# Two hybrid mixers in which turning, evicting and splitting weights change places

## The chip, the cores and the metric

One NeuronCore of a Trainium2 chip runs the whole kernel. The metric is the device time of one execution in microseconds (us). Engines are called by the names of the profile: PE (TensorE), DVE (VectorE), ACT (ScalarE), POOL (GpSimd) and SP (SyncE, which issues the large transfers).

## The reference, cut to what matters

The input is 256 tokens of width 1024 and passes four layers, two of a first kind and two of a second. The change touches only the mixer of the first kind, which runs twice (l = 0 and l = 1; here mixer 0 and mixer 1):

```python
def hybrid_mixer(h, ...):
    proj = h @ w_in                     # 256 x 2216
    z, xs, bm, cm, dt, q_lat, kv_lat, k_pe, gu, gv = split(proj)
    xs, bm, cm = split(silu(causal_depthwise_conv(concat(xs, bm, cm)) + conv_b))
    dt = softplus(dt + dt_bias)
    y_ssd = gated_group_rmsnorm(ssd_scan(xs, bm, cm, dt, a_log, d_skip), z, ssd_norm_w)
    q = rms_norm(q_lat, q_norm) @ w_qb          # then rope on its last 32 of 96
    kv = rms_norm(kv_lat, kv_norm) @ w_kvb      # 4 heads, 64 keys and 64 values each
    y_mla = mla_attention(q, kv, rope(k_pe))    # causal, 4 heads
    y_gm = gelu(gu) * (tril(w_s) @ layer_norm(gelu(gv)) + b_s)
    return concat(y_ssd, y_mla, y_gm) @ w_out
```

Behind mixer 0 comes a dense feed-forward (SwiGLU), behind mixer 1 eight experts of which each token uses two. Then come the two layers of the second kind.

## The kernel before

**Weights.** All weights stream in blocks of 1 MB through a ring of six slots (`plan`, `NS = 6`). SP issues the transfer of block n as soon as the last use of block n - 6 is over, strictly in the order of the plan. Products are made in three parts from numbers split in two: ACT copies a block to its high half (`high_halves`, L1261, ring of three), DVE subtracts that from the block and has the low half (`low_halves`, L1944), written over the block itself, and PE multiplies high by high, high by low and low by high (L497 to L499). Modulation vectors (`ada_w` blocks) are not split: DVE multiplies and adds them (`gemv`, L1884, two instructions for each block), and does so in `low_halves` ahead of the first split block that follows them in the plan. Four of them in mixer 0 are taken by PE (`gate_block`, L525).

**Order.** There is no planner: each engine has a program written out by hand and runs it in order. A wait on a semaphore stands in front of an instruction and holds all that is queued behind it on that engine. `ahead(i)` is the block two after i, so each block's step splits the weights two blocks ahead.

**A mixer.** The columns of `w_in` come as blocks named by their first column: 1280, 1536 (time steps, latents, k_pe), 512, 768, 1024 (the features xs, bm, cm, transposed), 1792, 2048 (gu, gv), 0, 256 (z). A token block makes tokens by columns, and ACT evicts it (`token_block`, L1405 and L1407). A feature block makes columns by tokens; ACT evicts it (L1415) and begins the convolution (L1423), DVE adds three taps for each of two chunks (L2188), ACT applies Silu (L1427). The latents are normalised on DVE, transposed by PE (`latents_turned`, L769), evicted by ACT (L1446), projected by PE (`latents_projected`, L779, L782) and evicted by ACT to q, k and v (L1455, L1459, L1460). DVE rotates them (`roped`, L2159), PE turns the heads (L795), and DVE and ACT copy two groups of them each (L2218, L1465). `differences` makes the decay matrices (PE L821, DVE L2296, ACT L1510).

**Attention.** It is a generator, and each `next(mla)` is one step in each engine's program: scores of head i (PE L724, L725), mask, maximum (DVE L2126 to L2132), exponentials (ACT L1390, L1391); probabilities of head i - 2 turned (PE L702) and evicted (ACT L1374); values of head i - 3 (PE L714 to L716). Between these steps stand the work of the scan (L2305, L2318, L2331, L848, L856), the gates (Gelu L1492 on ACT; statistics, root and normalisation one half of the tokens after the other, L2258 to L2268 on DVE, L1266 on ACT) and the last input blocks. At the end PE transposes the gated and attended part (L579), for which the last thing needed is L2311 on DVE, and multiplies it by two blocks of `w_out` in full (L886), while DVE and ACT finish the scan's part.

**PSUM.** Four banks (`R`) are taken in turn by block products, turned latents, projections, turned heads, scores and so on (`psum`); whoever takes a bank waits until its holder four takes earlier is evicted ("free"). Three more (`R2`) serve decays and turned inputs in the same way.

Of the kernel before, what the change touches and what calls it, by code (L numbers as in the profile page):

```python
# [8 lines left out]
ALU = mybir.AluOpType  # L9
# [78 lines left out]
def hybrid_kernel(nc, a, out):  # L88
    ctx = ExitStack()
    with ctx:  # L90
# [384 lines left out]
        def tensor_program(pe):  # L475
# [254 lines left out]
            def mixer1(l, m):  # L730
# [514 lines left out]
        def scalar_program(act):  # L1245
# [149 lines left out]
            def mixer1(l, m):  # L1395
# [3 lines left out]
                def token_block(c0, n):  # L1399
                    high_halves(main, ahead(turn_of["win", l, c0]))  # L1400
                    summed(turn_of["win", l, c0])
                    act.wait_ge(*at(*M, "token", c0))
# [6 lines left out]
                def feature_block(c0):  # L1409
                    high_halves(main, ahead(turn_of["win", l, c0]))  # L1410
                    summed(turn_of["win", l, c0])
# [10 lines left out]
                    for k in (ch, ch + 1):  # L1422
                        act.activation(xv[:, k, :], xc[:, k, 0:256], ACT.Identity, bias=pA[:, pc + 24 + k:pc + 25 + k], scale=pA[:, pc + k:pc + k + 1]).then_inc(  # L1423
                            *main.act((*M, "conv begun", k)))
                    for k in (ch, ch + 1):
                        act.wait_ge(*at(*M, "conv", k))
                        act.activation(xv[:, k, :], xv[:, k, :], ACT.Silu).then_inc(*main.act((*M, "xv", k)))  # L1427
# [62 lines left out]
                def gates():  # L1490
                    act.wait_ge(*main.act.last())
                    act.activation(G2[:, :, :], P1[:, :, 424:936], ACT.Gelu).then_inc(*main.act((*M, "gelu")))  # L1492
                    for t in range(2):
                        sd((*M, "gv", t), stat(2, *M, "gv mv", t)[:, 1:2])
# [34 lines left out]

                token_block(1280, 256)  # L1530
                time_steps()
                token_block(1536, 256)
# [329 lines left out]
        def vector_program(dve):  # L1862
# [302 lines left out]
            def mixer1(l, m):  # L2165
# [87 lines left out]
                def gates():  # L2253
                    dve.wait_ge(*at(*M, "gelu"))
                    for t in range(2):
                        bs, mv = stat(6, *M, "gv bs", t), stat(2, *M, "gv mv", t)
                        gv = G2[:, t, 256:512]
                        dve.bn_stats(bs, gv).then_inc(*vec())  # L2258
                        settled()
                        dve.bn_aggr(mv, bs).then_inc(*vec())  # L2260
                        rstd((*M, "gv", t), mv[:, 1:2], 1, 1e-5)
                        settled()
# [822 lines left out]
```

## Time and profile before

| | us |
|---|---|
| median of 3 runs | 2162.19 (2161.97 to 2172.66) |
| the profiled execution | 2158.98 |
| its span in the profile | 2157.1 |
| PE busy | 1985.6 (92%) |
| DVE busy | 1678.9 (78%) |
| ACT busy | 1169.0 (54%) |

Mixer 0 lies at about 42 to 190 us, mixer 1 at about 430 to 560 us of the span. The page's slices show PE busy 6 to 8 tenths in parts of these and 9 in most others. The granted clock of PE is 1.00 at full speed and 0.50 at its lower level.

### The profile page before, as it was taken

Reading aid. Unit: us, or ns where it says so; the run is one execution under the profiler, and the core shown is the slowest. Engines: PE = TensorE matmul, PEld = TensorE weight load, DVE = VectorE, ACT = ScalarE, POOL = GpSimd, SP = SyncE. Lnnn points to the kernel's source line nnn. Section 1 sums busy time; section 2 is a strip of 40 time slices with the busy share of each in tenths; the row PEclk is TensorE's granted clock in tenths of the full one; section 3 lists DMA queues with packets and bytes.
Section 4 is the critical chain, followed back from the end, with each engine's and each line's share of the span. In section 5 each row is a group of like instructions: output and inputs, shape, how many; then the busy total and the mean of one; then the engine's idle time right before and its main releaser. Section 6 shows DMA issues by size and latency. Waiting matters only on the chain.

```text
span 2157.1 us, 28343 instructions
## 1 busy us (share of the span) xinstructions
PE 1985.6 (92%) x11530; PEld 1717.5 (80%) x11530; DVE 1678.9 (78%) x1765; ACT 1169.0 (54%) x1314; POOL 73.3 (3%) x121
## 2 busy tenths in 40 slices
PE   6878999978889999999999999967889999889999
PEld 6676898777568787888788888757779998779998
DVE  6675888877588889898889989889678896865444
ACT  3543334364367777777677767645553345655432
POOL 6001000000100000000000000000010000000000
PEclk9988999998899999999999999978889999989999
DMA  9743799842389999999999999937229995314552
GB/s 353 244 166 137 278 335 370 285 130 99 138 285 323 350 366 366 332 349 375 343 342 355 370 331 358 343 101 248 86 97 338 353 368 182 121 59 137 187 184 98
DMA packets 251208, 554.37 MB, mean 257 GB/s; under 512 B 10076, under 2 KB 75856, under 8 KB 251072
## 3 DMA queue, kind: packets, MB, share of 16 engines
q1 hardware_dynamic: 247252, 544.13, 70.8%
q0 software_dynamic: 3552, 8.29, 1.1%
q8 instruction: 94, 1.54, 0.3%
q14 instruction: 42, 0.34, 0.1%
q10 hardware_dynamic: 268, 0.07, 0.0%
HBM read 551.40 MB, written 1.05 MB: 256 GB/s over the span
## 4 chain that ended last, share of the span: by engine, by line
PE 71%; DVE 14%; ACT 7%; issue 4%; DMA 4%; SPq 0%; ACTq 0%; DVEq 0%
PE bank L497 21%; PE bank L498 21%; PE bank L499 21%; DVE ring_lo L1944 4%; ACT ring_hi L1261 3%; DMA ring<-in_w_in_dram 1%; PE bank L886 1%; DVE acc L1884 1%; DMA ring<-in_ada_w_dram 1%; PE bank L579 1%; PE bank L1086 1%; DVE XN L2188 1%; DMA ring<-in_ffn_w_dram 1%; DVE work L2126 1%; PE bank L548 0%
## 5 line engine op out<-in xcount | busy, mean ns | idle before, releaser
L1944 DVE TENSOR_TENSOR ring_lo<-ring,ring_hi 128x2048 fp32r<-128x2048 f32 x417 | 950.1, 2286 | 271.4 <-ACT ring_hi L1261 268.4
L1261 ACT ACTIVATE ring_hi<-ring 128x2048 fp32r<-128x2048 f32 x417 | 795.5, 1913 | 492.0 <-PE bank L499 240.6
L497 PE MATMUL bank<-hh,ring_hi 128*128 128x256 f32 x1152 | 332.9, 289 | 19.5 <-ACT QK L1455 8.8
L498 PE MATMUL bank<-hl,ring_hi 128*128 128x256 f32 x1152 | 330.8, 287 | 0.0
L499 PE MATMUL bank<-hh,ring_lo 128*128 128x256 f32 x1152 | 330.5, 287 | 0.0
L497 PE MATMUL bank<-ring_hi,hh 128*128 128x256 f32 (+2 forms) x672 | 219.4, 327 | 30.6 <-ACT PT L1405 10.0
L497 PEld LDWEIGHTS bank<-hh,ring_hi 128*128 128x128 f32 x1152 | 226.2, 196 | 24.2 <-issue 13.5
L499 PE MATMUL bank<-ring_hi,hl 128*128 128x256 f32 (+2 forms) x768 | 241.9, 315 | 0.0
L497 PE MATMUL bank<-ring_hi,hgh 128*128 128x512 f32 (+1 forms) x576 | 220.3, 382 | 8.9 <-DVE ring_lo L1944 3.5
L498 PEld LDWEIGHTS bank<-hl,ring_hi 128*128 128x128 f32 x1152 | 226.2, 196 | 0.7 <-issue 0.2
L499 PEld LDWEIGHTS bank<-hh,ring_lo 128*128 128x128 f32 x1152 | 226.1, 196 | 0.0
L499 PE MATMUL bank<-ring_hi,hgl 128*128 128x512 f32 (+1 forms) x576 | 216.3, 375 | 0.0
L498 PE MATMUL bank<-ring_lo,hgh 128*128 128x512 f32 (+1 forms) x576 | 216.2, 375 | 0.0
L498 PE MATMUL bank<-ring_lo,hh 128*128 128x256 f32 (+2 forms) x672 | 212.9, 317 | 0.0
L497 PE MATMUL bank<-ring_hi,uh 128*128 128x512 f32 x496 | 199.0, 401 | 7.0 <-DVE ring_lo L1944 5.9
L498 PE MATMUL bank<-ring_lo,uh 128*128 128x512 f32 x496 | 196.5, 396 | 0.0
L499 PE MATMUL bank<-ring_hi,ul 128*128 128x512 f32 x496 | 196.5, 396 | 0.0
L1884 DVE SCALAR_TENSOR_TENSOR acc<-ring,csil,acc 128x1024 f32<-128x1024 f32 x140 | 179.8, 1284 | 13.7 <-DMA ring<-in_ada_w_dram 7.4
L497 PEld LDWEIGHTS bank<-ring_hi,hh 128*128 128x128 f32 x672 | 140.0, 208 | 47.0 <-issue 35.8
L499 PEld LDWEIGHTS bank<-ring_hi,hl 128*128 128x128 f32 x768 | 154.9, 202 | 6.6
L498 PEld LDWEIGHTS bank<-ring_lo,hh 128*128 128x128 f32 x672 | 140.3, 209 | 5.0 <-issue 0.7
L497 PEld LDWEIGHTS bank<-ring_hi,hgh 128*128 128x128 f32 x576 | 108.1, 188 | 33.8 <-issue 4.7
(424 smaller groups left out, 2774.4 us busy)
## 6 DMA issues: line engine op xcount, KB each, us to landing
ring<-in_moe_w_dram SPq DMA_DIRECT2D x264, 1024.0 KB, 5.2
ring<-in_ada_w_dram SPq DMA_DIRECT2D x48, 1024.0 KB, 7.2
ring<-in_w_mod_dram SPq DMA_DIRECT2D x48, 1024.0 KB, 7.3
ring<-in_w_in_dram SPq DMA_DIRECT2D x40, 1024.0 KB, 6.3
ring<-in_ffn_w_dram SPq DMA_DIRECT2D x33, 1024.0 KB, 5.5
ring<-in_w_gate_dram SPq DMA_DIRECT2D x22, 1024.0 KB, 5.1
ring<-in_w_up_dram SPq DMA_DIRECT2D x22, 1024.0 KB, 5.1
ring<-in_w_down_dram SPq DMA_DIRECT2D x22, 1024.0 KB, 5.0
```

The source lines that it names most:

```text
L497: pe.matmul(ps, xh, wh, start=first, stop=False)
L498: pe.matmul(ps, xh, wl, start=False, stop=False)
L499: return pe.matmul(ps, xl, wh, start=False, stop=last)
L579: x = pe.transpose(ban[kk][:, 256 * i + 128 * t:256 * i + 128 * t + 128], src[:, t, 128 * kc:128 * kc + 128], ident)
L886: x = pe.matmul(Y[t][h][:, :], YT[:, 2 * i + k, 128 * t:128 * t + 128], w[:, c:c + 512], start=first and k == 0, stop=False)
L1086: x = pe.transpose(ps[:, 128 * c:128 * c + 128], U[:, 128 * c:128 * c + 128], ident)
L1261: act.activation(ring_hi[i % NH][:, 0:z], ring[n % NS][:, 0:z], ACT.Copy).then_inc(*s.hi(("hi", home(s, i), i)))
L1884: x = dve.scalar_tensor_tensor(v, w[:, k, :], csil[:, col:col + 1], v, ALU.mult, ALU.add)
L1944: dve.tensor_tensor(ring_lo[n % NS][:, 0:z], ring[n % NS][:, 0:z], hi, ALU.subtract).then_inc(*s.lo(("lo", home(s, i), i)))
L2126: dve.tensor_tensor(S, R.of(*A, "scores", i, c)[:, 0:384], mask, ALU.add).then_inc(*vec(("free", *A, "scores", i, c)))
L2188: dve.scalar_tensor_tensor(xv[:, k, :], xc[:, k, j:j + 256], col(j), xv[:, k, :], ALU.mult, ALU.add).then_inc(*vec((*M, "conv", k)))
```

## The change

Only the orders inside `mixer1` change, on PE, ACT and DVE, and the gates' normalisation.

- PE: `latents_turned` stands behind block 768 and `latents_projected` behind block 1024 and its gate block; block 1792 stands ahead of `heads_turned`.
- ACT: the eviction is separate from the splitting (`block`) and from the Silus (`feature_gates`). Block 768 is split ahead and evicted before the latents, block 1024 before the projections; each pair of Silus comes after these. Block 1792 comes ahead of the heads. The high halves that stood with blocks 2048, 0 and 256 (those of blocks 256, and of `w_out` 0 and 1) come later.
- DVE: `roped` stands behind the decays; `block("win", 1792)` ahead of the copies of the heads; `block("win", 2048)` two attention steps later; the blocks 0 and 256 behind the gates, the spatial weights and the first chunk's output.
- Gates: both halves of the tokens together, in two parts, `gates_spread` up to the variance and `gates` from the root on; one root on ACT for two columns.

```diff
@@ PE, mixer1
                 feature_block(512)
                 gate_block(1)
-                latents_turned()
                 feature_block(768)
                 gate_block(2)
-                latents_projected()
+                latents_turned()
                 feature_block(1024)
                 gate_block(3)
+                latents_projected()
                 decays()
                 differences(0)
+                token_block(1792, 256)
                 heads_turned()
-                token_block(1792, 256)
@@ ACT, mixer1: block(c0) is now its own function, taken out of token_block
+                def block(c0):
+                    high_halves(main, ahead(turn_of["win", l, c0]))
+                    summed(turn_of["win", l, c0])
...
                 feature_block(512)
+                feature_gates(512)
+                feature_block(768)
                 latents_turned()
-                feature_block(768)
+                feature_gates(768)
+                feature_block(1024)
                 latents_projected()
-                feature_block(1024)
+                feature_gates(1024)
                 decays()
                 differences(0)
+                block(1792)
+                token_block(1792, 256)
                 heads_turned()
-                token_block(1792, 256)
...
                 next(mla)
                 contents()
                 next(mla)
+                block(2048)
                 gates()
                 states()
                 token_block(0, 256)
                 next(mla)
+                block(0)
+                sd((*M, "gv"), stat(4, *M, "gv mv")[:, 1:4:2])
                 token_block(256, 256)
+                block(256)
                 next(mla)
@@ DVE, mixer1
+                def gates_spread():
+                    mv = stat(4, *M, "gv mv")
                     dve.wait_ge(*at(*M, "gelu"))
                     for t in range(2):
...
+                        x = dve.bn_stats(stat(6, *M, "gv bs", t), G2[:, t, 256:512])
...
+                        x = dve.bn_aggr(mv[:, 2 * t:2 * t + 2], stat(6, *M, "gv bs", t))
...
+                    dve.tensor_scalar(mv[:, 1:4:2], mv[:, 1:4:2], 1e-5, None, ALU.add).then_inc(*vec((*M, "gv", "var")))
+                def gates():
+                    mv, gv = stat(4, *M, "gv mv"), G2[:, :, 256:512]
+                    dve.wait_ge(*at(*M, "gv", "sd"))
+                    dve.reciprocal(mv[:, 1:4:2], mv[:, 1:4:2]).then_inc(*vec())
...
+                    dve.tensor_tensor(gv, gv, bc(gmr[:, 0, :].unsqueeze(1), [128, 2, 256]), ALU.mult).then_inc(*vec())
...
+                    dve.tensor_tensor(gv, gv, bc(gmr[:, 1, :].unsqueeze(1), [128, 2, 256]), ALU.add).then_inc(*vec((*M, "gv", 0), (*M, "gv", 1)))
...
                 feature_block(768)
-                roped()
                 feature_block(1024)
                 decays()
+                roped()
                 differences(0)
+                block("win", 1792)
                 heads_turned()
-                block("win", 1792)
                 mla = attention((*M, "mla"), mla_heads(l), MLA_SCALE)
                 next(mla)
                 differences(1)
                 next(mla)
-                block("win", 2048)
                 stepped_inputs()
                 next(mla)
                 decayed(0)
                 next(mla)
+                block("win", 2048)
                 skipped_inputs()
+                decayed(1)
+                gates_spread()
+                next(mla)
                 gates()
+                spatial_weights()
+                chunk_outputs(0)
                 block("win", 0)
-                decayed(1)
-                next(mla)
-                spatial_weights()
                 block("win", 256)
-                chunk_outputs(0)
                 next(mla)
```

## Rows read from the trace of the kernel before

**Rows 1.** The page: busy us, share of the span; then two costly groups of instructions.

```profile
PE 1985.6 (92%) x11530; PEld 1717.5 (80%) x11530; DVE 1678.9 (78%) x1765; ACT 1169.0 (54%) x1314; POOL 73.3 (3%) x121
...
L1944 DVE TENSOR_TENSOR ring_lo<-ring,ring_hi 128x2048 fp32r<-128x2048 f32 x417 | 950.1, 2286 | 271.4 <-ACT ring_hi L1261 268.4
```

**Rows 2.** Order of time, PE, mixer 0: start, duration, instruction, [idle before <- releaser].

```profile
88.48 0.55 PE L497 MATMUL bank<-hh,ring_hi 128*128 128x256 f32 x1 [4.39 <-ACT QK L1455]
...
108.82 0.55 PE L497 MATMUL bank<-ring_hi,hh 128*128 128x256 f32 x1 [3.74 <-DVE QK L2218]
...
115.96 0.38 PE L724 MATMUL bank<-QK 96*128 96x128 f32 x2
...
134.59 0.69 PE L714 MATMUL bank<-QK,work 128*128 128x64 f32 x2 [6.46 <-ACT work L1374]
...
154.03 0.55 PE L497 MATMUL bank<-ring_hi,hh 128*128 128x256 f32 x1 [4.16 <-ACT PT L1405]
...
169.69 1.81 PE L579 MATMUL bank<-cst,YK 128*128 128x128 f32 x8 [1.26 <-DVE YK L2311]
```

**Rows 3.** Order of time, PE, mixer 1.

```profile
470.58 0.55 PE L497 MATMUL bank<-hh,ring_hi 128*128 128x256 f32 x1 [4.39 <-ACT QK L1455]
...
485.27 0.36 PE L497 MATMUL bank<-ring_hi,hh 128*128 128x256 f32 x1 [3.17 <-DVE QK L2218]
...
491.10 0.39 PE L724 MATMUL bank<-QK 96*128 96x128 f32 x2
...
520.70 0.55 PE L497 MATMUL bank<-ring_hi,hh 128*128 128x256 f32 x1 [5.88 <-ACT PT L1405]
...
535.73 1.51 PE L579 MATMUL bank<-cst,YK 128*128 128x128 f32 x6 [1.26 <-DVE YK L2311]
```

**Rows 4.** Order of time, ACT, mixer 0, first part.

```profile
87.54 0.42 ACT L1427 ACTIVATE XN<-XN 128x256 f32<-128x256 f32 x1 [1.02 <-DVE XN L2188]
87.86 0.47 ACT L1455 ACTIVATE QK<-bank 128x384 f32<-128x384 f32 x1
...
89.66 1.36 ACT L1261 ACTIVATE ring_hi<-ring 128x1344 fp32r<-128x1344 f32 x1
100.06 0.69 ACT L1276 ACTIVATE gate<-bank,cst 128x512 f32<-128x512 f32 x1 [9.04 <-PE bank L531]
```

**Rows 5.** Order of time, DVE, mixer 0, first part.

```profile
89.30 0.90 DVE L2159 TENSOR_TENSOR PT<-QK,cst 128x128 f32<-128x128 f32 x4 [1.79 <-ACT QK L1455]
...
91.77 2.60 DVE L1884 SCALAR_TENSOR_TENSOR acc<-ring,csil,acc 128x1024 f32<-128x1024 f32 x2
...
102.76 2.96 DVE L2188 SCALAR_TENSOR_TENSOR XN<-YT,pA,XN 128x256 f32<-128x256 f32 x6 [6.92 <-ACT XN L1423]
...
105.93 2.15 DVE L2296 SCALAR_TENSOR_TENSOR gate<-bank,st,cst 128x128 f32<-128x128 f32 x8
108.00 1.27 DVE L2218 COPY QK<-bank 96x512 f32<-96x512 f32 x2
109.19 5.30 DVE L1884 SCALAR_TENSOR_TENSOR acc<-ring,csil,acc 128x1024 f32<-128x1024 f32 x4
```

**Rows 6.** Order of time, ACT, mixer 0, second part.

```profile
131.91 1.91 ACT L1261 ACTIVATE ring_hi<-ring 128x2048 fp32r<-128x2048 f32 x1 [8.16 <-DMA ring<-in_w_in_dram]
...
144.70 1.28 ACT L1492 ACT_TABLE_LOAD   x1
145.99 1.06 ACT L1492 ACTIVATE PT<-PT 128x1024 f32<-128x1024 f32 x1
```

**Rows 7.** Stretches, DVE alone: us, busy (instructions), PE's granted clock, DMA share, GB/s.

```profile
138.00:169.60 31.60, 20.24 (x43) 0.82 0.41 150
504.90:535.70 30.80, 22.61 (x45) 0.88 0.32 111
```

**Rows 8.** Stretches, PE alone: us, busy (instructions), granted clock, DMA share, GB/s.

```profile
110.00:113.00 3.00, 3.00 (x21) 0.70 0.00 0
155.00:158.00 3.00, 3.00 (x16) 0.50 0.94 320
```

More of the change, by code:

```diff
@@ L1409, in feature_block @@
                 def feature_block(c0):
-                    high_halves(main, ahead(turn_of["win", l, c0]))
-                    summed(turn_of["win", l, c0])
+                    block(c0)
                     ch = (c0 - 512) // 128
@@ L1424, in feature_block, with feature_gates @@
                             *main.act((*M, "conv begun", k)))
+                def feature_gates(c0):
+                    ch = (c0 - 512) // 128
                     for k in (ch, ch + 1):
@@ L1492, in gates @@
                     act.activation(G2[:, :, :], P1[:, :, 424:936], ACT.Gelu).then_inc(*main.act((*M, "gelu")))
-                    for t in range(2):
-                        sd((*M, "gv", t), stat(2, *M, "gv mv", t)[:, 1:2])
                 def decays():
@@ L1528, in out_block @@
                     summed(turn_of["wout", l, i])
+                block(1280)
                 token_block(1280, 256)
                 time_steps()
+                block(1536)
                 token_block(1536, 256)
@@ L2251, in time_steps_after @@
                     dve.scalar_tensor_tensor(av_, dt_, -1.0, bc(sstat[:, 80:88].unsqueeze(1), [128, 2, 8]), ALU.mult, ALU.mult).then_inc(*vec((*M, "a")))
-                def gates():
+                def gates_spread():
+                    mv = stat(4, *M, "gv mv")
                     dve.wait_ge(*at(*M, "gelu"))
                     for t in range(2):
[L2256 to L2262, printed above, removed]
-                        dve.tensor_scalar(gv, gv, mv[:, 0:1], mv[:, 1:2], ALU.subtract, ALU.mult).then_inc(*vec())
-                        settled()
-                        dve.wait_ge(*at("ws", l))
-                        dve.tensor_tensor(gv, gv, gmr[:, 0, :], ALU.mult).then_inc(*vec())
-                        settled()
-                        dve.tensor_tensor(gv, gv, gmr[:, 1, :], ALU.add).then_inc(*vec((*M, "gv", t)))
+                        x = dve.bn_stats(stat(6, *M, "gv bs", t), G2[:, t, 256:512])
+                    x.then_inc(*vec())
+                    settled()
+                    for t in range(2):
+                        x = dve.bn_aggr(mv[:, 2 * t:2 * t + 2], stat(6, *M, "gv bs", t))
+                    x.then_inc(*vec())
+                    settled()
+                    dve.tensor_scalar(mv[:, 1:4:2], mv[:, 1:4:2], 1e-5, None, ALU.add).then_inc(*vec((*M, "gv", "var")))
@@ new lines, in gates @@
+                def gates():
+                    mv, gv = stat(4, *M, "gv mv"), G2[:, :, 256:512]
+                    dve.wait_ge(*at(*M, "gv", "sd"))
+                    dve.reciprocal(mv[:, 1:4:2], mv[:, 1:4:2]).then_inc(*vec())
+                    settled()
+                    for t in range(2):
+                        x = dve.tensor_scalar(gv[:, t, :], gv[:, t, :], mv[:, 2 * t:2 * t + 1], mv[:, 2 * t + 1:2 * t + 2], ALU.subtract, ALU.mult)
+                    x.then_inc(*vec())
+                    settled()
+                    dve.wait_ge(*at("ws", l))
+                    dve.tensor_tensor(gv, gv, bc(gmr[:, 0, :].unsqueeze(1), [128, 2, 256]), ALU.mult).then_inc(*vec())
+                    settled()
+                    dve.tensor_tensor(gv, gv, bc(gmr[:, 1, :].unsqueeze(1), [128, 2, 256]), ALU.add).then_inc(*vec((*M, "gv", 0), (*M, "gv", 1)))
```

2 lines of the change are left out of this document (1 added, 1 removed).

## The prediction

> **What bounds the kernel now.** I read the page first, then the waits and the order of time of PE, ACT and DVE in the two first mixers. PE is busy 92% of the span [rows 1], so what can be won lies where it waits. In the first mixer it waits 4.39 us before the block at 88.48 (for ACT's eviction of q), 3.74 before 108.82 (for DVE's copy of the turned heads), 6.46 before 134.59 (for ACT's eviction of turned probabilities), 4.16 before 154.03 (for ACT's eviction of the z block) [rows 2]. The second mixer has three of them: 4.39, 3.17 and 5.88 [rows 3]; the 6.46 is missing there, as its weights are in time. None is work that PE lacks. Each is an in-order queue: ACT's eviction stands behind an activation that waits for DVE (the Silu at 87.54, 1.02 after its convolution was asked for, and only then the q eviction at 87.86, whose bank the block at 88.48 takes [rows 4]), or behind weight splitting: ACT's high halves at 131.91 waited 8.16 us for the transfer of the last input block, and all behind them on ACT waited too [rows 6]. Behind such waits PE's clock falls as well: granted 0.70 in 110 to 113 us and 0.50 in 155 to 158, which is 1.2 GHz [rows 8].
>
> The two mixers are each a chain in two parts, cut at the first scores of the attention (115.96 and 491.10 [rows 2, 3]). I call that moment T and follow the new order from row to row. All work behind a mixer (boundary, feed-forward, experts) is unchanged; its transfers are gated by slots of the ring that PE frees, so I let a gain pass on in full.
>
> **First part, mixer 0.** The feature block 768 comes before the turning of the latents, so by bank order (four banks taken in turn) block 1024 needs the bank of block 512, evicted long before, and no longer that of q: the 4.39 goes. PE runs 768 at 68.4, gate block, turning, 1024 from 78.5 to 84.3, gate block and its sums to 89.6, projections to 94.2 and block 1792 from about 96.6 to 102.4, which before ended at 116.1. PE is no more the bound. What is late next is ACT and DVE:
> - ACT: the high halves of 1792 end at about 81.0 (0.9 us earlier than before, as block 768 ends 0.8 earlier), eviction and the two first conv steps to 82.7, latents to 83.8, then the Silus of 768, which end at 88.0 as before since DVE's convolution sets them. High halves of 2048, 1.36, to 89.4 [rows 4]; two gate evictions of 0.7 (before they waited 9.04 for PE [rows 4]) to 90.8; block 1024 evicted, conv begun, 92.5; six evictions of q and kv, 2.4, to 95.0.
> - DVE: the convolution of 1024, 2.96, ran at 102.76 after 6.92 of waiting [rows 5]; now 91.9 to 94.8. Decay copies 0.6. The rotation, 89.30 to 91.77 [rows 5] = 2.5, now behind it: 98.0. Differences 2.15 [rows 5]: 100.1. Now the change puts the low halves of block 0 in front of the copies of the turned heads, and in front of those stand four modulation products, 5.30 [rows 5], and the halves, 2.29 [rows 1]: 107.7. Copies 1.27: 108.9.
>
> So T comes at 108.9 instead of 115.96: **7.1 us gained**. The 3.74 stall is replaced by one of 5 us before T, in which PE has nothing. Bounds for this term: if the four products were hidden, T would be 105 (block 1792 to 102.4, transposes 1.5, copy 1.3), 11 gained; if DVE's convolution were not earlier, T would be 119.6, 3.7 lost.
>
> **First part, mixer 1.** The same order, no gate blocks, two modulation products fewer in it. Silu of 768 ends at 470.0 as before; high halves 1.36, eviction and conv begun: 473.1; convolution of 1024 473.0 to 475.9; copies to 476.4; rotation 478.9; differences 481.0. ACT's exponentials of the differences end at 481.6, its high halves of block 0 (1.9) at 483.5, so DVE waits 2.5 us, low halves to 485.8, copies 487.1. The last key transpose waits also, for ACT's eviction of block 1792 behind these halves (484.2). T is 487.1 instead of 491.10: **4.0 us**. The 4.39 and 3.17 stalls go, and PE idles some 5 us ahead of T instead.
>
> **Second part.** Counted from T. Before, the gated output that PE's next transposes wait for (DVE, L2311) was done at 53.6 in mixer 0 (169.6) and at 44.5 in mixer 1 (535.6) [rows 2, 3]. Now:
> - Scores, differences and inputs turned need the same time; block 2048 ends at 10.0 (before at 126.0, likewise). ACT evicts it and the turned probabilities at once, since the high halves of block 256 stand two steps later: the 6.46 goes. Third mask at 11.0 instead of 22.0 in mixer 0.
> - ACT: exponentials of head 3 end at 17.9; high halves of block 256 (landed at 16, as before) 19.8; Gelu with its table load (1.28 + 1.06 [rows 6]) 22.2; states and the z block evicted by 23.2: PE, ready at 23.0, hardly waits, so the 4.16 and 5.88 go.
> - DVE is now the bound. From the third mask to the gated output it had 20.24 us of work in mixer 0 and 22.61 in mixer 1 [rows 7]. To that come the products and low halves moved behind the masks: 5.3 + 2.3 in mixer 0, 2.6 + 2.3 in mixer 1. The gates in one go save some 0.6 (ten instructions for fourteen, the last two of them 512 wide) and one round trip to ACT. Sums: 27.2 and 26.9. Waits in it: 2.0 for the contents evicted behind exponentials; for the root 0.3 in mixer 0, and 2.1 in mixer 1, where DVE asks at 25.9 and ACT has first the high halves of the output block (which land at 24.6) to 26.5, then 1.28 of table and 0.2; seams of 0.05 between dependent instructions, 1.0. From 11.0: **41.2 and 43.0**. Gains: 53.6 - 41.2 = 12.4 and 44.5 - 43.0 = 1.5.
>
> The last low halves of the output blocks (4.6 us) stay in front of the second chunk's output as they were; PE will stand there 4 to 6 us for L2311. Nothing behind hides it. The second half of the SSD path has 10 us of cover by the 32 products of L886, in the old order as in the new.
>
> **Clock.** New idle stretches of PE: some 5 us before T in both mixers, 4 and 6 us before the transposes of L579 where 1.26 stood [rows 2]. After 4 us of idling 155 to 158 ran at half [rows 8]: 1.5 us lost there for that window alone. Bounds for one such place: 0, as behind the 3.17 wait, where the next block ran at full speed, and 3.5. I take 1.8 at each T (it delays block 2048, on which the rest hangs), 1.0 and 0.5 more than before at L579: 5.1 in all. What is saved of low clock in the middle is inside the difference to 53.6 already.
>
> The Trainium skill, "TensorE: Matmul & The Clock Gate", What's actually happening, says that the throttled clock is the default state and activity releases it. By this rule idling moved is idling paid again, which speaks against this change; the trace agrees with 0.50 [rows 8]. Were each of the four stretches paid in full the gain would be 6 smaller.
>
> A load of tables before Gelu took 1.28 and the Gelu began 0.01 later (144.70, 145.99) [rows 6]. The Trainium skill, "ScalarE: Activation LUTs", What ACT_TABLE_LOAD costs, puts a switch of sets at about 2.66 us with its drain. By it the root would come 1.4 later in each mixer and the gain be 2.8 smaller; I go by the row. The count of loads stays the same.
>
> **Sum.** 7.1 + 4.0 + 12.4 + 1.5 = 25.0; less clock 5.1; less 2 for handoffs between engines that I stepped over, some twenty at 0.1: 18 us. The profiled execution took 2158.98 (span 2157.1), the median of the runs is 2162.19. The difference is between executions; I take the gain off the median: **2144**.
>
> **Rivals.**
> - A, part of it given back: DVE's new order (low halves ahead of copies) plus low clock eat the first part whole, and the second keeps 12.4 - 4. Then 7 to 9 us: 2154. For it: every moved wait has DVE behind it, at 78% busy over the kernel. Against: DVE idled 6.92 ahead of the convolution [rows 5], and it waited on ACT's 8.16 [rows 6] too: the work moved has these holes to go to.
> - B, more: the first part goes to its upper bound in mixer 0, since the slots free earlier, and clock costs little: 25 + 4 = 29: 2133.
> - C, slower: the queue of DVE before T. If the convolution of 1024 does not come earlier (a transfer of block 2048 or the gate evictions later than I have them; it decides at DVE's 102.76 against 91.9), rotation, differences, four products, low halves and copies in a row put T at 119.6, 3.7 later, and by the same sum 2.3 later in mixer 1 (convolution at 479.2 as before, T 493.4). With two deeper clock falls of 3.5 that is 13 lost; if then the halves of block 256 land as late as before and DVE has 7.6 more behind them, the second part gains nothing: 2175. Against: nothing in the new order feeds the convolution but block 1024, whose bank is free.
> - D, it doesn't do what it says: the wait for block 256's transfer (8.16) just moves to where its product stands, so that mixer 0's second part gains 6, not 12: 2150. Against: the new order asks for these halves at 17.9 after T and the transfer lands at 16.
>
> **Chances.** Forecast with its surroundings (2137 to 2150) 0.58; A 0.17; B 0.10; D 0.11; C 0.04. The range: 2136 to 2156. What counts as no change is within 0.5%, 10.8 us, so 2151.4 to 2173: that is A, part of the forecast's upper edge and of D: 0.18; slower 0.03; faster 0.79.
>
> **What would show it.** In the trace after: no wait of PE for L1455 and none of 6 us at L714; block 1792 before the heads; T near 109 and, in mixer 1, near 472 (487.1 less the 15 to 16 gained in mixer 0, 19.5 less its share of clock and handoffs); the L1405 waits under 1 us; new waits of PE for L2218 or the scores and, at L579, for L2311 of 4 to 6 us; granted clock 0.5 to 0.7 just behind T. Wrong it would be if ACT's high halves of block 2048 start later than 90, if DVE waits for an arrival before its four products, or if the masks of head 3 come later than 19 after T.

## The result, and the profile after

The changed kernel takes 2138.22 us (median of 4 runs, 2136.80 to 2143.60) against 2163.98 (4 runs) for the kernel before: ratio 0.9891, 95% interval 0.9873 to 0.9909, so some 24 us faster. I had forecast 2144 and a range of 2136 to 2156. The profiled execution is the slowest of the four: 2143.60 us, span 2141.8; against the profiled 2158.98 of before that is 15.4 less. The profiled execution of the kernel before is in turn faster than all four of its timed ones (2161.97 to 2172.66). The two medians lie 25.8 apart: 5.0 us of the gap come from the profiled execution before, 5.4 from the one after. Where those 5.4 went is asked below.

The line numbers of DVE and ACT have moved in the changed kernel: L2230 is L2218 of before (copies of the turned heads), L2334 is L2311 (gated output), L2354 is L2331 (addition of a chunk's output, `chunk_outputs`), L1956 is L1944 (low halves), L1896 is L1884 (modulation products).

PE's order of time in mixer 0 answers to [rows 2] (start, duration, instruction, [idle before <- releaser]). The waits of 4.39, 3.74, 6.46 and 4.16 us are gone; the first scores, T, come at 108.77 instead of 115.96 behind a new wait of 5.22, and the transposes L579 at 153.25 instead of 169.69.

```profile
102.91 0.31 PE L795 MATMUL bank<-cst,QK 128*96 128x128 f32 x1 [0.35 <-ACT PT L1409]
...
108.77 0.77 PE L724 MATMUL bank<-QK 96*128 96x128 f32 x2 [5.22 <-DVE QK L2230]
...
110.61 3.10 PE L821 MATMUL bank<-cst,sstat 128*128 128x128 f32 x14
...
134.87 0.39 PE L497 MATMUL bank<-ring_hi,hh 128*128 128x256 f32 x1 [1.03 <-DVE ring_lo L1956]
...
143.18 2.77 PE L848 MATMUL bank<-YT,gate 128*128 128x64 f32 x16 [1.36 <-DVE YK L2354]
...
148.37 3.62 PE L872 MATMUL bank<-PT 128*128 128x64 f32 x16
153.25 1.94 PE L579 MATMUL bank<-cst,YK 128*128 128x128 f32 x8 [1.26 <-DVE YK L2334]
```

PE in mixer 1, to [rows 3]. Where the waits of 4.39, 3.17 and 5.88 were, there is one of 3.08 before a projection, which the prediction did not have, one of 1.06 before T and one of 2.35 before L848. A fourth wait of before, 4.11 us at 452.64 for the normalised latents (DVE L2198), which the prediction did not count, has become one of 1.38 at 447.82 and one of 1.90 at 455.74. T to L579 is 43.3 us, before 44.6.

```profile
462.50 2.08 PE L782 MATMUL bank<-mlaw,PT 128*128 128x512 f32 x2 [3.08 <-ACT YT L1416]
...
477.51 0.46 PE L724 MATMUL bank<-QK 96*128 96x128 f32 x2 [1.06 <-DVE QK L2230]
...
509.83 3.68 PE L848 MATMUL bank<-YT,gate 128*128 128x64 f32 x16 [2.35 <-DVE YK L2354]
...
520.81 1.94 PE L579 MATMUL bank<-cst,YK 128*128 128x128 f32 x8 [1.26 <-DVE YK L2334]
```

DVE ahead of T in mixer 0, to [rows 5]: convolution of block 1024, rotation (from 95.28), differences, four modulation products, low halves, copies, without a hole.

```profile
92.10 2.96 DVE L2200 SCALAR_TENSOR_TENSOR XN<-YT,pA,XN 128x256 f32<-128x256 f32 x6
...
95.28 0.89 DVE L2171 TENSOR_TENSOR PT<-QK,cst 128x128 f32<-128x128 f32 x4
...
97.75 2.15 DVE L2319 SCALAR_TENSOR_TENSOR gate<-bank,st,cst 128x128 f32<-128x128 f32 x8
99.82 5.30 DVE L1896 SCALAR_TENSOR_TENSOR acc<-ring,csil,acc 128x1024 f32<-128x1024 f32 x4
105.04 2.28 DVE L1956 TENSOR_TENSOR ring_lo<-ring,ring_hi 128x2048 fp32r<-128x2048 f32 x1
107.24 1.28 DVE L2230 COPY QK<-bank 96x512 f32<-96x512 f32 x2
```

DVE at the end of mixer 0's row, ahead of L579: here it waits for PE.

```profile
152.03 1.12 DVE L2334 SCALAR_TENSOR_TENSOR YK<-bank,pA,PT 128x128 f32<-128x128 f32 x4 [1.67 <-PE bank L872]
```

DVE's busy time from the third mask to the gated output in each mixer, to [rows 7] (us, busy, PE's granted clock, DMA share, GB/s). It was 20.24 and 22.61; forecast 27.2 and 26.9.

```profile
121.70:153.20 31.50, 26.48 (x43) 0.86 0.70 251
488.60:520.80 32.20, 26.49 (x43) 0.82 0.36 131
```

PE's granted clock in the changed kernel in four stretches of mixer 0, to [rows 8]: it is 0.50 (1.2 GHz) behind the wait before T, again low behind the 1.36 before L848, and still low at L872 and up to L579.

```profile
109.00:112.00 3.00, 3.00 (x13) 0.50 0.00 0
112.00:115.00 3.00, 3.00 (x21) 0.75 0.00 0
...
144.00:147.00 3.00, 3.00 (x15) 0.53 0.92 331
150.00:153.00 3.00, 1.99 (x10) 0.50 0.00 0
```

### The profile page after: what moved, and what is told of

Same layout as the page of the kernel before. It is cut to its first block, busy times and chain, and to the rows that moved or that the text cites. A ratio compares the mean times of both kernels' runs of the same rounds, so it can differ in the third digit from the quotient of the medians.

```text
span 2141.8 us, 28331 instructions
## 1 busy us (share of the span) xinstructions
PE 1985.2 (93%) x11530; PEld 1716.7 (80%) x11530; DVE 1676.3 (78%) x1757; ACT 1169.2 (55%) x1312; POOL 72.7 (3%) x121
## 4 chain that ended last, share of the span: by engine, by line
PE 70%; DVE 14%; ACT 7%; DMA 5%; issue 4%; SPq 0%; ACTq 0%; DVEq 0%
PE bank L497 21%; PE bank L498 20%; PE bank L499 20%; DVE ring_lo L1956 4%; ACT ring_hi L1261 4%; DMA ring<-in_ffn_w_dram 2%; DVE acc L1896 1%; PE bank L886 1%; DMA ring<-in_w_in_dram 1%; DMA ring<-in_ada_w_dram 1%; PE bank L579 1%; PE bank L1086 1%; DVE XN L2200 1%; PE bank L548 1%; DVE work L2138 1%
## 5 line engine op out<-in xcount | busy, mean ns | idle before, releaser
L1956 DVE TENSOR_TENSOR ring_lo<-ring,ring_hi 128x2048 fp32r<-128x2048 f32 x417 | 950.0, 2286 | 270.5 <-ACT ring_hi L1261 267.8
L1896 DVE SCALAR_TENSOR_TENSOR acc<-ring,csil,acc 128x1024 f32<-128x1024 f32 x140 | 179.7, 1283 | 14.2 <-DMA ring<-in_ada_w_dram 7.7
```

The source lines that it names most:

```text
L1896: x = dve.scalar_tensor_tensor(v, w[:, k, :], csil[:, col:col + 1], v, ALU.mult, ALU.add)
L1956: dve.tensor_tensor(ring_lo[n % NS][:, 0:z], ring[n % NS][:, 0:z], hi, ALU.subtract).then_inc(*s.lo(("lo", home(s, i), i)))
```

## The experiments

All times are medians, each ratio is against the kernel before on the same chip in the same session (its median there was 2162.15 to 2163.98; the table has that of the first). The columns from the fourth on come from one profiled execution each. "T" and "L579" are read from PE's order of time as above. The table gives all runs; "FF" is the stretch from the feed-forward's first product to mixer 1's first.

| run | median us | ratio (95%) | T, mixer 0 | T to L579, mixer 0 | FF | T to L579, mixer 1 |
|---|---|---|---|---|---|---|
| before | 2163.98 | | 115.96 | 53.73 | 218.9 | 44.63 |
| changed | 2138.22 | 0.9891 (0.9873-0.9909) | 108.77 | 44.48 | 225.0 | 43.30 |
| first part only | 2150.99 | 0.9942 (0.9921-0.9964) | 108.07 | 56.85 | 217.9 | 45.52 |
| second part only | 2152.93 | 0.9949 (0.9930-0.9968) | 116.76 | 42.05 | 221.7 | 43.05 |
| changed again | 2140.39 | 0.9887 (0.9871-0.9904) | 108.33 | 44.15 | 220.6 | 45.93 |
| chunk first | 2137.04 | 0.9877 (0.9860-0.9895) | 107.74 | 42.08 | 219.1 | 43.02 |
| both late | 2127.13 | 0.9831 (0.9813-0.9848) | 109.00 | 39.79 | 220.0 | 38.64 |
| late lows | 2134.77 | 0.9863 (0.9841-0.9884) | 109.48 | 40.27 | 221.5 | 44.38 |
| ten products | 2137.52 | 0.9883 (0.9863-0.9903) | 112.34 | 41.92 | 217.4 | 42.99 |
| heads first | 2145.83 | 0.9923 (0.9897-0.9948) | 104.62 | 53.07 | 222.9 | 44.74 |
| spread | 2124.78 | 0.9824 (0.9811-0.9838) | 107.21 | 41.56 | 220.6 | 36.26 |
| five products | 2137.62 | 0.9888 (0.9872-0.9903) | 108.13 | 42.07 | 218.7 | 44.09 |
| old gates | 2144.74 | 0.9916 (0.9903-0.9930) | 108.38 | 47.07 | 222.5 | 47.54 |

**First part only.** Up to `heads_turned` the changed order, from T on that of the kernel before.

Against the changed kernel, with the functions `gates` of the kernel before and, on ACT, each `block` back inside its token block, ahead of the eviction:

```diff
 ACT             contents()
                 next(mla)
-                block(2048)
                 gates()
                 states()
                 token_block(0, 256)
                 next(mla)
-                block(0)
-                sd((*M, "gv"), stat(4, *M, "gv mv")[:, 1:4:2])
                 token_block(256, 256)
-                block(256)
...
 DVE             next(mla)
+                block("win", 2048)
                 stepped_inputs()
                 next(mla)
                 decayed(0)
                 next(mla)
-                block("win", 2048)
                 skipped_inputs()
+                gates()
+                block("win", 0)
                 decayed(1)
-                gates_spread()
                 next(mla)
-                gates()
                 spatial_weights()
-                chunk_outputs(0)
-                block("win", 0)
                 block("win", 256)
+                chunk_outputs(0)
```

> Only the first part of the change: latents turned and projected a block later, evictions ahead of the Silus, rotation behind the decays, block 1792 ahead of the heads; from the first scores on all is as before, high and low halves of block 256 too. Theory (the two parts are separate gains cut at the first scores T): T comes 7.2 us earlier in mixer 0 (108.8) and 4.3 more in mixer 1, as in the changed kernel; T to PE's transposes stays 53.7 and 44.6 us, with the waits of 6.5 (L714) and 4 to 6 (L1405) back. Gain 10 to 12 us, ratio about 0.995. Rival (the parts hang together, the second is what lets the first through, or the transfer of block 256 eats it): gain under 5.

**Second part only.** The reverse: the order of before up to the heads, the changed one behind. Against the changed kernel:

```diff
 PE              gate_block(1)
+                latents_turned()
                 feature_block(768)
                 gate_block(2)
-                latents_turned()
+                latents_projected()
                 feature_block(1024)
                 gate_block(3)
-                latents_projected()
                 decays()
                 differences(0)
-                token_block(1792, 256)
                 heads_turned()
+                token_block(1792, 256)
...
 ACT             feature_gates(512)
-                feature_block(768)
                 latents_turned()
+                feature_block(768)
                 feature_gates(768)
-                feature_block(1024)
                 latents_projected()
+                feature_block(1024)
                 feature_gates(1024)
                 decays()
                 differences(0)
+                heads_turned()
                 block(1792)
                 token_block(1792, 256)
-                heads_turned()
...
 DVE             feature_block(768)
+                roped()
                 feature_block(1024)
                 decays()
-                roped()
                 differences(0)
-                block("win", 1792)
                 heads_turned()
+                block("win", 1792)
```

> Only the second part: halves two steps later on ACT and DVE, gates together; up to the heads all is as before. Theory: T stays at 116 in mixer 0; T to the transposes of L579 falls from 53.7 to about 43 in mixer 0 (the changed kernel had 44.5 with PE cold for some 1.8 us behind T, which here has the block 1792 ahead of it) and from 44.6 to about 43 in mixer 1. Gain 11 to 13 us, ratio about 0.9945. Rival (the gain of the second part came from the first part's earlier release of ring slots): T to L579 stays above 49 in mixer 0, gain under 6.

Measured: 0.9942 and 0.9949; the two shortfalls, 0.0058 and 0.0051, add to 0.0109, and the whole change has 0.0109 and, again, 0.0113. By the times they are separate gains of about equal size, as the theory had it. The waits of the second part are back in the first run, 6.39 us at L714 and 4.50 and 5.87 at L1405. Beyond the forecast: with the first part alone T to L579 in mixer 0 grew from 53.73 to 56.85, and with the second alone it fell to 42.05, lower than the 44.48 of both. So the first part's earlier T goes with 2.1 to 3.1 us more behind T. The granted clock points at the cause: with the second part alone it is 1.00 behind T, where the changed kernel has 0.50. The runs with added products test that.

```profile
117.00:120.00 3.00, 3.00 (x26) 1.00 0.62 180
```

In mixer 1 this run has a cost that the table does not show: from its first product to T it took 63.3 us, 2.8 more than the kernel before with the same order there. The waits are all but the same (4.09, 4.39 and 3.17), but the clock behind them differs: 0.54 in 477.8 to 480.8 behind the 3.17, against 1.00 in 485.3 to 488.3 in the kernel before.

**The changed kernel again.**

> The changed kernel once more, for its spread. In the two profiles at hand the products of mixer 0 end 16.4 us earlier, yet mixer 1 begins only 9.3 earlier: 7 us went in the dense feed-forward between them. Theory (the loss is the transfers' own variation from execution to execution): the stretch from the first product of the feed-forward to the first of mixer 1, 218.9 us in the trace before and 225.0 in the one after, is near 219 in this one. Rival (a price of the change: the feed-forward is bound by transfers and cannot be entered earlier): it is near 225 again. Time 2137 to 2140 either way, ratio 0.989.

Mixer 1 differs between the two executions of the changed kernel. In the first PE waits 1.06 us before T and runs at 1.00 behind it, the second scores come 2.52 us behind T, and T to L579 is 43.30. In this one it waits 2.60, runs at 0.50, the second scores come 4.83 behind T, and T to L579 is 45.93.

```profile
472.31 0.77 PE L724 MATMUL bank<-QK 96*128 96x128 f32 x2 [2.60 <-DVE QK L2230]
```

PE's stretches behind T in mixer 1, this execution and, below, the first one of the same kernel:

```profile
472.30:475.30 3.00, 2.98 (x12) 0.50 0.00 0
...
477.50:480.50 3.00, 2.99 (x24) 1.00 0.53 216
```

FF is 220.6, neither 219 nor 225. Over all thirteen profiles it lies between 217.4 and 225.0, and 225.0, that of the changed kernel's first profile, is the largest. Kernels with mixer 0 even shorter (both late) have 220.0. A price of the change of 6 us in every execution is ruled out by that; a price of 1 to 2 us can't be excluded, as the one profile of the kernel before has 218.9. That the variation is the transfers' own is argued, not shown.

**Chunk first.**

```diff
                 next(mla)
-                gates()
                 spatial_weights()
                 chunk_outputs(0)
+                gates()
                 block("win", 0)
```

> The changed kernel with spatial_weights and chunk_outputs(0) ahead of gates on DVE, where DVE waits for the root (1.04 us in mixer 0, 3.01 in mixer 1). Theory (PE's waits of 1.36 and 2.35 us for L2354 and the low clock behind them come from the bank that chunk_outputs(0) frees late): these waits go, L848 behind them takes 1.95 instead of 2.77 and 3.68, and the transposes of L579 come 1 to 3 us earlier in mixer 0 (where DVE had waited 1.67 for L872) and about 1.3 in mixer 1, where DVE's row of work stays the bound. Gain over the changed kernel 2 to 4 us. Rival (DVE's total is all that counts): 0 to 1.

The wait before L848 went and L848 ran in 1.95; instead PE stood 3.51 us at L579, so DVE's row of work is the next bound. From the start of L848 to the end of L872 PE took 5.2 us, in the changed kernel 8.8. T to L579 is 2.1 to 2.4 shorter than in the changed kernel in mixer 0. In mixer 1, where the second scores came 4.16 behind T (low clock), the 43.02 is to be held against the 45.93 rather than the 43.30: some 2.9 shorter, with PE standing 6.86 at L579. 0.9877 against 0.9887 in the same session: not told apart by timing.

```profile
141.12 1.95 PE L848 MATMUL bank<-YT,gate 128*128 128x64 f32 x16
...
149.82 1.94 PE L579 MATMUL bank<-cst,YK 128*128 128x128 f32 x8 [3.51 <-DVE YK L2334]
```

**Both late, and late lows alone.** Both late is chunk first and this (there `gates()` stands between `chunk_outputs(0)` and the two blocks):

```diff
                 chunk_outputs(0)
-                block("win", 0)
-                block("win", 256)
                 next(mla)
                 chunk_outputs(1)
...
                 late_features()
+                block("win", 0)
+                block("win", 256)
                 outputs()
```

> As the run with spatial_weights and chunk_outputs(0) ahead of the gates, and in addition the low halves of the two w_out blocks (and in mixer 1 the two modulation products ahead of them) stand on DVE behind late_features, not ahead of the second chunk's output. Theory (DVE's row of work up to L2311's place is what the transposes of L579 wait for, 3.5 us in mixer 0 and 6.9 in mixer 1 in that run): L579 comes 3 to 4.5 us earlier in mixer 0 and 5.5 to 7 in mixer 1, and the 32 products of L886 cover the 4.5 and 7.1 us moved behind. Gain over that run 8 to 11 us, ratio to the kernel before about 0.983. Rival (the cover is too short, the second transposes then wait for the scan's part): under 3 us.

> The changed kernel with only the low halves of the w_out blocks behind late_features; chunk_outputs(0) stays behind the gates. Theory: DVE is freed of 4.5 and 7.1 us, but PE's second within_chunk still waits for chunk_outputs(0) with the low clock behind it, so L579 moves 1 us or less earlier in mixer 0 (there DVE had already waited 1.67 for PE) and 1 to 3 in mixer 1. Gain 1 to 4 us over the changed kernel. Rival (DVE's total work is the bound alone): 4 and 7 us.

Both late has the time that was forecast, 0.9831, 10 us under chunk first, but not quite the terms. T to L579 is 2.3 shorter than in chunk first in mixer 0 (forecast 3 to 4.5) and 4.4 in mixer 1 (5.5 to 7); the rest came behind L579, where mixer 1 took 39.9 us up to its next stage instead of 43.0. The cover of L886 sufficed. Late lows alone gained 5 to 6 us by the ratio, above the forecast of 1 to 4. T to L579 is 40.27 in mixer 0, 4 us shorter, as its rival said: PE waited 1.07 us before L848, yet its clock stayed at 1.00, and L848 and L872 took 2.00 and 1.95 (in the changed kernel 2.77 and 3.62). Why the clock stayed up there is not shown. In mixer 1 it is 44.38: the late `chunk_outputs(0)` held PE for 2.73 us and L848 took 3.20. So in mixer 0 late lows do nearly all that both edits do (40.27 against 39.79); in mixer 1 it takes both (38.64).

**Ten products, five products.** Idle PE is kept busy before T:

```diff
                 heads_turned()
+                for _ in range(10 if l == 0 else 2):      # five products: 5 and 0
+                    pe.matmul(Y[0][0][:, :], ident, cst[:, 0:512], start=True, stop=True)
                 mla = attention((*M, "mla"), mla_heads(l))
```

> The changed kernel with products of 128x512 put on PE between the turned heads and the scores, ten in mixer 0 and two in mixer 1, written to a bank that nobody reads then; they add work, the outputs stay. Theory (idling before T costs low clock behind it, 2.4 us by the difference of 42.05 to 44.48 us from T to L579 between the run of the second part alone and the changed kernel): in mixer 0 the scores and differences behind T run at full clock, T to L579 is near 42, gain 2 us in the kernel. Rival (the 2.4 us came from elsewhere, such as DVE's row): T to L579 stays near 44.3.

> The changed kernel with five products of 128x512 on PE between the turned heads and the scores in mixer 0 only (they add work, the outputs stay), 0.87 us each by the run with ten, so that they end at 107.5 to 108, before T. Theory (low clock behind T costs 2.4 us): T stays at 108.3 to 108.8, the differences behind it take 1.95 us instead of 3.10, T to L579 is near 42. Gain 2 us over the changed kernel, which its timing alone hardly shows. Rival: T to L579 near 44.3.

Ten took 8.7 us (0.87 each) and ended behind the old T, so T came late, 112.34, but T to L579 fell to 41.92. Five ended in time: T 108.13, T to L579 42.07, the value of the second part alone, the differences L821 took 1.95 us, and the second scores came 2.52 us behind T instead of 4.78. In mixer 1, with the two products of the first of these runs in front of T, the second scores came 2.44 behind T.

```profile
108.13 0.46 PE L724 MATMUL bank<-QK 96*128 96x128 f32 x2 [0.49 <-DVE QK L2232]
...
108.86 1.95 PE L821 MATMUL bank<-cst,sstat 128*128 128x128 f32 x16
```

```profile
109.00:112.00 3.00, 3.00 (x28) 1.00 0.00 0
```

So work that nobody needs buys back 2.1 to 2.4 us (44.48 and 44.15 to 42.07): that is the price of low clock behind T in mixer 0. In the median it does not show (0.9888).

**Heads first.** On DVE:

```diff
                 differences(0)
-                block("win", 1792)
                 heads_turned()
+                block("win", 1792)
```

> The changed kernel with the two orders of block 1792 and the copies of the turned heads swapped on DVE. Theory (DVE's row, not T, is the bound in mixer 0): T comes 4 to 4.6 us earlier, at 104.2, but the first mask, which stands behind the four modulation products and the low halves, still comes at 110.5 to 111; L579 moves by less than 1 us either way in both mixers. Rival (T sets the end, as the sum of the prediction had it with its bound of 11 instead of 7 us): 4 us gained in mixer 0.

T came 4.15 earlier, as both expected, and the first mask at 111.47, half a microsecond behind what my theory had. But the kernel got slower than the changed one, by 5 to 8 us (0.9923 against 0.9887 and 0.9891; the intervals just overlap, and L579 of mixer 0 came 4.4 to 5.2 later in the profile), which neither had: PE, scores done, came to the transposes of the inputs and waited 5.56 us for a bank that DVE frees in `differences(1)`, behind the same products. Block 2048 then ran at half clock (granted 0.50 in each stretch from 115 to 127, with PE busy throughout), and all behind it was late. In the changed kernel DVE does the same products before T, and PE's wait is the one of 5.22 there.

```profile
104.62 0.46 PE L724 MATMUL bank<-QK 96*128 96x128 f32 x2 [0.77 <-ACT QK L1469]
...
113.96 1.11 PE L830 MATMUL bank<-cst,XN 128*128 128x128 f32 x4 [5.56 <-DVE gate L2319]
```

**Spread.** Both late, and in mixer 0 DVE's two products in front of the heads' copies go behind the second mask:

```diff
                 differences(0)
+                if l == 0:
+                    low_halves(main, ahead(turn_of["win", l, 1792]), False)   # without gemv
                 block("win", 1792)
                 heads_turned()
...
                 next(mla)
+                if l == 0:
+                    gemv(mods_left.pop(0))
                 stepped_inputs()
+                if l == 0:
+                    gemv(mods_left.pop(0))
                 next(mla)
```

> The best run so far (low halves of w_out late, chunk_outputs(0) ahead of the gates) and, in mixer 0 only, the two modulation products of DVE (four instructions, 5.3 us) taken out from in front of the copies of the turned heads: low halves of block 0 first, one product before stepped_inputs, one behind it, where DVE waited 1.5 and 2.0 us. Theory (these products set T in mixer 0 and PE's idling there costs clock behind it): T at 103.5 to 104 instead of 109.0, PE waits for L2230 under 1 us instead of 5.2, third mask 3 to 5 us earlier, L579 near 144 instead of 148.8. Gain 4 to 5 us over that run, about 2123. Rival (DVE's total is the bound and swallows it, as when the copies alone went ahead): under 1.5.

T came at 107.21, not at 103.5 to 104: DVE now waited 2.50 us for ACT's high halves of block 0, which stand behind ACT's exponentials, so the 5.3 us taken out brought T only 1.8 forward. L579 stayed (148.77 against 148.79). The 0.9824 against 0.9831 is inside the intervals, though it is the fastest median, 2124.78. The rival has the number right, but not the reason: at the end DVE waited 3.22 us for PE (L848), so its total was not the bound. PE began block 256 1.5 us earlier than in both late, but behind a wait of 2.39 instead of 1.03, at a granted clock of 0.63 instead of 1.00, and ended it at the same time (the next transposes start at 141.38, in both late at 141.40).

```profile
103.47 2.29 DVE L1956 TENSOR_TENSOR ring_lo<-ring,ring_hi 128x2048 fp32r<-128x2048 f32 x1 [2.50 <-ACT ring_hi L1261]
```

PE at the start of block 256, and its stretch behind that, in spread; the last line is the same place in both late:

```profile
134.04 0.39 PE L497 MATMUL bank<-ring_hi,hh 128*128 128x256 f32 x1 [2.39 <-DVE ring_lo L1956]
```

```profile
134.00:137.00 3.00, 2.96 (x16) 0.63 1.02 403
...
135.50:138.50 3.00, 2.95 (x24) 1.00 1.02 412
```

In mixer 1 the two kernels are the same, and T to L579 was 36.26 here and 38.64 in both late: the second scores came 2.51 behind T here and 4.83 there. That is the low clock behind T once more, 2.4 us.

**Old gates.** The functions `gates` of the kernel before at the new place, with a root for each half:

```diff
 ACT             block(0)
-                sd((*M, "gv"), stat(4, *M, "gv mv")[:, 1:4:2])
+                for t in range(2):
+                    sd((*M, "gv", t), stat(2, *M, "gv mv", t)[:, 1:2])
...
 DVE             decayed(1)
-                gates_spread()
                 next(mla)
                 gates()
```

> The changed kernel with the gates' normalisation as before, one half of the tokens after the other, in the place of the new one. Theory of the prediction (grouping saves 0.6 us of DVE's work and one round trip to ACT): DVE's stretch from the statistics to the last addition, 4.7 us in mixer 0 and 6.6 in mixer 1 in the changed kernel, grows by 2 to 3 us in each, and the transposes of L579 come 2 to 3 us later in each mixer; 4 to 6 us slower than the changed kernel. Rival (the root only waits behind ACT's high halves, with or without grouping): under 2.

T to L579 was 47.07 and 47.54, 2.6 to 2.9 and 1.6 to 4.2 longer than in the two profiles of the changed kernel; 0.9916 against 0.9887 and 0.9891, 5 to 6 us (the intervals just overlap). By these numbers grouping is about a quarter of the whole gain. The second trip to ACT explains little of it: DVE waited 0.27 us for it in each mixer. From the statistics to the last addition DVE took 6.0 us in mixer 0 instead of 4.7, so 1.3 more where 2 to 3 were forecast, 1.0 of it work and the seams of more instructions. The rest came through PE: it waited 2.69 us before L848 instead of 1.36, L848 took 3.21, the clock was 0.58 in 145 to 148 and 0.50 in 148 to 151, and DVE waited 2.12 for L872. In mixer 1 ACT's high halves ahead of the root waited 3.31 us for their transfer, 1.93 and 2.19 in the changed kernel, so part of the difference there is not the edit's.

## Why the prediction was right, and where not

- **T, mixer 0.** Forecast 108.9, measured 108.77, and by the chain as written: eviction and gate evictions earlier, then DVE's row without a hole. The bound of 105 for hidden products was wrong in kind: without them ACT's high halves are next (spread), and with the copies alone in front PE waits a step later (heads first).
- **T, mixer 1.** From its first product to T 60.5 before, 56.2 now: 4.3 gained, forecast 4.0. The step for PE failed, though: the last projection waited 3.08 us for the bank of block 1024, whose eviction the new order puts behind the Silus of 768. I had followed the bank only for block 1024 itself. It cost nothing in T, since DVE's row was later still: in all nine profiles with this order ahead of T, T came 56.2 to 56.3 us behind mixer 1's first product, with that wait at 3.07 or 3.08 in six of them and at 1.38 in three. In absolute time T was forecast near 472; it came at 477.51 in the first profile, with 6 us of that lost in FF, and at 472.31 in the second.
- **Second part.** The waits at L714 and L1405 went. L579 at 44.5 after T in mixer 0 (forecast 41.2 with 1.8 and 1.0 of clock, 44.0) and 43.3 in mixer 1 (43.0 with 2.3, 45.3). DVE's work was 26.5 in both for 27.2 and 26.9. The terms listed for mixer 0 add up to 41.5, not 41.2, so 12.1 gained and not 12.4. DVE waited 1.04 and 3.01 for the root, where I had 0.3 and 2.1: ACT's high halves ahead of it waited for the transfer of the output block in both mixers (2.21 and 1.93). A root ahead of these halves was not tried. The 43.3 is of the execution with full clock behind T; with low clock it was 45.93, so that mixer 1 agrees with 45.3 only when the clock falls, as I had charged it.
- **L579.** I had PE standing there 4 to 6 us for L2311. It stood 1.26, which in mixer 0 is little more than L2334 itself (1.12), begun when PE's own L872 was done. The step that failed is that PE arrives early: it waited before L848 for the bank that `chunk_outputs(0)` frees, and ran the rest at half clock (L848 2.77 and 3.68 for 1.95, L872 3.62 for 1.95), so that in mixer 0 DVE even waited 1.67 for PE. Chunk first brought PE's wait back, 3.51 and 6.86. The forecast of the whole hardly felt this miss, as DVE's row ended about where I had it.
- **Clock.** 1.8 at each T: 2.1 to 2.4 in mixer 0, shown by filling the idle time. In mixer 1 it varies between executions: of the nine profiles with the same order ahead of T, three ran the scores behind it at full clock (second scores 2.5 us behind T) and six wholly or partly at half (4.05 to 4.83); two pairs of equal code (spread and both late, the changed kernel twice) differ by 2.4 and 2.6 us from T to L579; five products, only partly at half clock there, has 0.8 more than the first of the changed kernel's two. The bound of 0, taken from the 3.17 wait, was one such case: behind the same wait the second part alone had 0.54. The other 1.5, charged at L579, fell due between L848 and L872 instead (3.6 us of PE in mixer 0 against chunk first). The "6 smaller" for all stretches paid in full has no sum behind it; at my bound of 3.5 a place, four places are 14, 8.9 more than charged. The granted clock in mixer 0 is 0.50 behind the wait and 1.00 with five products in it. The Trainium skill, "TensorE: Matmul & The Clock Gate", What's actually happening, takes the throttled clock as the default that activity releases; both rows agree with it.
- **Gates.** 0.6 us and a round trip, forecast inside the 12.4 and 1.5: worth 5 to 6 us of the kernel, of which the second round trip is 0.27 in each mixer and work and seams 1.0 in mixer 0; most of the rest is PE waiting longer and running at low clock behind that.
- **Sum.** The mixers gained 7.2 + 9.25 and 4.3 + 1.3 = 22.0 us in the two first profiles; the terms less clock were 25.0 - 5.1 = 19.9. The 2 us for handoffs were not needed. Of these 22 some 6 were lost in FF in that one execution, which is why its span fell only by 15.3; the medians, 24 by the ratio, are the better measure. Part of the 22 is luck: in the changed kernel's second profile, with low clock behind T in mixer 1, mixer 1 gained 3.0 instead of 5.6. So the mixers gained 20 to 22, the kernel 24, and I had forecast 18; where the last 2 to 4 us come from is open. Rivals A, C and D did not occur: the first part kept its gain, the convolution came at 92.10, and the high halves of block 256 waited for no transfer. Nor did B: T stayed at 108.8 and not 105.

## What to carry to other kernels

When an engine's wait moves, follow every PSUM bank taken in turn through the new order, not only the one that stalled before: the new waits of 3.08 us before a projection, of 1.36 and 2.35 before L848 and of 5.56 in heads first were all for banks freed later by the new order. Work on the bound engine that is needed much later (low halves of a block two steps ahead) belongs behind what PE waits for, if long products cover it there; that alone brought 0.9863 against 0.9887, and 0.9831 together with the bank freed in time. Two small steps on two halves are worth grouping where PE waits behind them, less for the trip to the other engine (0.27 us here) than for what PE's longer wait sets off. An earlier start of an engine is worth nothing if only a longer wait lies in front of it: look at the granted clock behind the wait before counting the gain (spread).

## What the runs showed of the hardware

A wait of 5.2 us before T cost PE a further 2.1 to 2.4 us behind it, and a fill of products with no other use gave that back. The wait of 1.36 us before L848 in mixer 0 was followed by a granted clock of 0.53 in 144 to 147; the tail of block 256 and the small products ran before it at 1.00 (PE busy 1.82 of the 3 us from 140 to 143).

The length of the last wait alone did not tell what the clock did. Behind 1.07 us before L848 it stayed at 1.00 in late lows (143 to 146), and L848 took 2.00; behind the same 1.07 it fell to 0.50 with five products (143 to 146), and L848 took 2.42. Behind 3.17 us before block 1792 in mixer 1 it was 1.00 in the kernel before and 0.54 with the second part alone. Behind T in mixer 1 the same kernel had 1.00 in one execution and 0.50 in another, which was 2.6 us up to L579. And behind the 5.56 of heads first it stayed at 0.50 for 12 us (115 to 127) though PE was busy all the time.

The same kernel took 225.0 and 220.6 us for the same feed-forward in two executions.
